# Softmax scores of a hybrid attention layer: float32 products replaced by three rounded products of split queries and keys

## The reference

```python
s = jnp.einsum('bhqd,bhkd->bhqk', q_blk, kh, preferred_element_type=jnp.float32) * scale
q_chunk = (blk * QBLOCK + jnp.arange(QBLOCK)) // CHUNK
mask = key_chunk[None, :] <= q_chunk[:, None]
p = jax.nn.softmax(jnp.where(mask, s, -1e30), axis=-1)
return jnp.einsum('bhqk,bhkv->bhqv', p.astype(vh.dtype), vh)
```

## Time and profile before

| | |
|---|---|
| median of 3 runs | 1137.3 us (1136.0 to 1137.32) |
| profiled execution | 1134.42 us |
| its span | 1132.3 us |
| TensorE busy | 1109.2 us (98%) |
| VectorE busy | 766.8 us (68%) |
| GpSimd busy | 529.7 us (47%) |
| ScalarE busy | 477.3 us (42%) |
| granted TensorE clock, mean | 0.998 |

### The profile page before, as it was taken

One profiled execution on the slowest core, in us unless ns is written; L12 is line 12 of the kernel. 1 busy time (PEld: TensorE's weight loads), 2 busy tenths in 40 slices (PEclk: granted clock), 3 DMA queues, 4 the chain that ended last, 5 costly groups with the idle time before them and its releaser, 6 DMA issues.

```text
span 1132.3 us, 14084 instructions
## 1 busy us (share of the span) xinstructions
PE 1109.2 (98%) x5094; PEld 874.6 (77%) x5094; DVE 766.8 (68%) x985; ACT 477.3 (42%) x869; POOL 529.7 (47%) x386
## 2 busy tenths in 40 slices
PE   7999999999999999999999999999999999999998
PEld 7978888764555558887888888888878888888887
DVE  5565767575575571288485775577798978888863
ACT  5353554426757562166323322332334434434341
POOL 2332613205475573047554444444545656555562
PEclk9999999999999999999999999999999999999999
DMA  7232523461221134223544234431789783456632
GB/s 255 66 130 75 168 85 112 108 164 36 75 62 52 57 115 164 75 86 101 177 142 138 101 112 139 139 113 38 262 276 377 236 285 121 135 192 216 208 116 84
DMA packets 101716, 158.37 MB, mean 140 GB/s; under 512 B 9360, under 2 KB 43232, under 8 KB 101648
## 3 DMA queue, kind: packets, MB, share of 16 engines
q1 hardware_dynamic: 100032, 152.83, 40.8%
q10 hardware_dynamic: 1296, 4.46, 1.1%
q0 software_dynamic: 320, 0.19, 0.2%
HBM read 115.47 MB, written 41.94 MB: 139 GB/s over the span
## 4 chain that ended last, share of the span: by engine, by line
PE 83%; DVE 8%; POOL 3%; issue 3%; DMA 2%; ACT 1%; SPq 0%; DVEq 0%; POOLq 0%; ACTq 0%
PE ps L2152 80%; POOL p_first L1022 1%; PE ps L2248 1%; DVE m_nm L1850 1%; DVE t_all L1924 1%; POOL tx_lo L1060 1%; DVE dr_lo L1924 1%; DMA up_raw<-in_w_up_dram 1%; DMA raw<-in_w_in_dram 1%; PE ps L2167 1%; POOL ua_lo L1065 1%; DMA m_ukv<-in_w_ukv_dram 0%; DVE stage L1924 0%; POOL a_lo L1060 0%; DVE xn L1564 0%
## 5 line engine op out<-in xcount | busy, mean ns | idle before, releaser
L2152 PE MATMUL ps<-dr_hi,dl_hi 128*128 128x512 f32 x448 | 174.5, 390 | 1.6 <-DVE dr_lo L1924 1.6
L2152 PE MATMUL ps<-dr_hi,dl_lo 128*128 128x512 f32 x448 | 174.3, 389 | 0.0
L2152 PE MATMUL ps<-dr_lo,dl_hi 128*128 128x512 f32 x448 | 174.3, 389 | 0.0
L1065 POOL TENSOR_TENSOR ua_lo<-up_raw,ua_hi 128x1024 fp32r<-128x1024 f32 x46 | 116.7, 2542 | 116.7 <-ACT ua_hi L1103 116.7
L1089 POOL TENSOR_TENSOR dl_lo<-l_raw,dl_hi 128x512 fp32r<-128x512 f32 x64 | 100.6, 1597 | 71.1 <-ACT dl_hi L1103 70.7
L1089 POOL TENSOR_TENSOR dl_lo<-s_all,dl_hi 128x512 fp32r<-128x512 f32 x48 | 75.2, 1586 | 58.2 <-ACT dl_hi L1103 57.5
L2152 PE MATMUL ps<-a_hi,ua_hi 128*128 128x512 f32 x256 | 99.9, 390 | 0.3 <-POOL ua_lo L1065 0.3
L2152 PEld LDWEIGHTS ps<-dr_hi,dl_hi 128*128 128x128 f32 x448 | 84.1, 188 | 20.1 <-issue 2.8
L2152 PE MATMUL ps<-a_hi,ua_lo 128*128 128x512 f32 x256 | 99.6, 389 | 0.0
L2152 PE MATMUL ps<-a_lo,ua_hi 128*128 128x512 f32 x256 | 99.6, 389 | 0.0
L2152 PEld LDWEIGHTS ps<-dr_lo,dl_hi 128*128 128x128 f32 x448 | 84.1, 188 | 17.5
(11 more groups left out here) (259 smaller groups left out, 2482.9 us busy)
## 6 DMA issues: line engine op xcount, KB each, us to landing
r_raw<-in_w_down_dram SPq DMA_DIRECT2D x144, 256.0 KB, 3.6
hidden<-stage SPq DMA_DIRECT2D x72, 256.0 KB, 2.1
up_raw<-in_w_up_dram SPq DMA_DIRECT2D x16, 1024.0 KB, 5.5
l_raw<-hidden SPq DMA_DIRECT2D x64, 256.0 KB, 3.5
raw<-in_w_in_dram SPq DMA_DIRECT2D x24, 256.0 KB, 3.4
z_gla<-z_stage SPq DMA_DIRECT2D x16, 256.0 KB, 2.0
raw<-in_w_out_dram SPq DMA_DIRECT2D x16, 256.0 KB, 3.3
xs<-in_x_dram SPq DMA_DIRECT2D x8, 512.0 KB, 7.3
```

What stands on the lines that cost most here:

```text
L1065: pool.tensor_tensor(ua_lo[n % UP_RING][:, :, :], up_source(g, product), ua_hi[n % UP_RING][:, :, :].bitcast(F32), ALU.subtract).then_inc( ...
L2152: return pe.matmul(dst, lhsT, rhs, start=start, stop=stop, skip_group_check=onto)
```

## The change

Scores are made of rounded factors. `m_q_hi` and `m_k_hi` get the 97th row (maxima and ones), `m_q` and `m_k` lose it, and in their place in memory stand `m_q_lo` and `m_k_lo` once the low parts are made. A score tile is three accumulated products: hi*hi with 97 rows, hi*lo and lo*hi with 96. Tiles of 128 queries are made 256 wide. The low parts are made by GpSimd (`mla_low`: four before `decays(0)`, and in step L0 of each pair but the last three for the next pair) and, for the queries of even units from the third on, by VectorE (`queries_low`, at step S1, place 2). A third row of ones is written by ScalarE. Of the odd unit's last three estimates, number 5 moves from place 0 of S0 to place 3 of the step L3 before it, number 6 stays at place 1, and number 7 goes from place 2 to place 3. The turn of the odd unit's maxima goes from S1 place 1 to place 2 for every pair, GLA part 1 (`gla_out`) from place 3 to place 2 of S0. Three pairs of semaphores are merged into single ones. The last denominators and the last GLA output go one block later into the output projection.

```diff
+        m_q, m_q_lo = ([at(f"{name}{n}", [DQK, 2, W], offset * KB, dt) for n, offset in enumerate((144, 168, 44, 60))]
+                       for name, dt in (("m_q", F32), ("m_q_lo", F32R)))
+        m_q_hi = [at(f"m_q_hi{n}", [DQK + 1, 2, W], offset * KB, F32R) for n, offset in enumerate((148, 200, 12, 28))]
...
-        ESTIMATES = {(S0, 0): (1, 5), (S0, 1): (1, 6), (S0, 2): (1, 7), (L0, 1): (2, 0), (L0, 3): (2, 1), (L1, 1): (2, 2),
-                     (L1, 2): (2, 3), (L2, 0): (3, 0), (L2, 1): (3, 1), (L2, 2): (3, 2), (L2, 3): (3, 3), (L3, 2): (3, 4)}
+        ESTIMATES = {(S0, 1): (1, 6), (S0, 3): (1, 7), (L0, 1): (2, 0), (L0, 3): (2, 1), (L1, 1): (2, 2),
+                     (L1, 2): (2, 3), (L2, 0): (3, 0), (L2, 1): (3, 1), (L2, 2): (3, 2), (L2, 3): (3, 3), (L3, 2): (3, 4),
+                     (L3, 3): (3, 5)}
...
-            if (d, place) == (1, 2):
-                return 1
-            if (d % 6, place) == (S1, 1) and d >= 6:
+            if (d % 6, place) == (S1, 2):
                 return 2 * (d // 6) + 1
...
-        GLA_AT = ((-1, 0, None, 1), (None, 2, None, None), (3, 4, None, 5), (6, 7, 8, 9), (10, 11, 12, None),
+        GLA_AT = ((-1, 0, 1, None), (None, 2, None, None), (3, 4, None, 5), (6, 7, 8, 9), (10, 11, 12, None),
...
+            def mla_low(kind, n):
+
+                pool.wait_ge(mla_hi, rounded(kind, n))
...
+                pool.tensor_tensor(at[:, :, some], whole[:, :, some], hi_at[0:DQK, :, some].bitcast(F32),
+                                   ALU.subtract).then_inc(m_lo_made, 1)
...
+            mla_low("k", 0)
+            mla_low("q", 0)
+            mla_low("k'", 0)
+            mla_low("q", 1)
             decays(0)
...
+                if t == L0 and p + 1 < MH // 2:
+                    mla_low("k", p + 1)
+                    mla_low("k'", p + 1)
+                    mla_low("q", 2 * p + 3)
...
+                if t == L1 and p == MH // 2 - 2:
+                    row_of_ones(2)
...
+            def queries_low(u):
+                n = queries_at(u)
+                dve.wait_ge(mla_hi, rounded("q", u))
+                for h in range(2):
+                    last = dve.tensor_tensor(m_q_lo[n][:, h, :], m_q[n][:, h, :], m_q_hi[n][0:DQK, h, :].bitcast(F32),
+                                             ALU.subtract)
+                last.then_inc(q_lo_made, 1)
...
+                    if (d % 6, place) == (S1, 2) and d // 6 + 1 < MH // 2:
+                        queries_low(2 * (d // 6) + 2)
...
-                seen = slice(first_query(j), W)
+                    pe.wait_ge(m_lo_made, LOW.index(("k'" if u % 2 else "k", p)) + 1)
+                    if ("q", u) in LOW:
+                        pe.wait_ge(m_lo_made, LOW.index(("q", u)) + 1)
+                    else:
+                        pe.wait_ge(q_lo_made, u // 2)
+                seen = slice(min(first_query(j), W - 2 * P), W)
+                some = slice(c * P, (c + 1) * P)
+                q, k = queries_at(u), keys_hi_at(p)
                 for s in range(2):
-                    last = mm(ps[:, score_bank(j) + s, seen], m_k[p % 2][:, s, c * P:(c + 1) * P],
-                              m_q[queries_at(u)][:, s, seen], True, True)
+                    to = ps[:, score_bank(j) + s, seen]
+                    mm(to, m_k_hi[k][:, s, some], m_q_hi[q][:, s, seen], True, False)
+                    mm(to, m_k_hi[k][0:DQK, s, some], m_q_lo[q][:, s, seen], False, False)
+                    last = mm(to, m_k_lo[p % 2][:, s, some], m_q_hi[q][0:DQK, s, seen], False, True)
...
-                    project(IN_GROUPS + n, pos, {(0, 0): last_sums, (0, 1): last_output}.get((n, pos)))
+                    project(IN_GROUPS + n, pos, {(0, 1): last_sums, (0, 2): last_output}.get((n, pos)))
```

More of the change, by code:

```diff
@@ L168, in layer @@
         m_v = at("m_v", [P, MH // 2, NB, 2 * MV], 128 * KB)
[L171 to L174, removed]
+        m_q, m_q_lo = ([at(f"{name}{n}", [DQK, 2, W], offset * KB, dt) for n, offset in enumerate((144, 168, 44, 60))]
+                       for name, dt in (("m_q", F32), ("m_q_lo", F32R)))
+        m_q_hi = [at(f"m_q_hi{n}", [DQK + 1, 2, W], offset * KB, F32R) for n, offset in enumerate((148, 200, 12, 28))]
+        m_k, m_k_lo = ([at(f"{name}{n}", [DQK, 2, T], offset * KB, dt) for n, offset in enumerate((152, 84))]
+                       for name, dt in (("m_k", F32), ("m_k_lo", F32R)))
+        m_k_hi = [at(f"m_k_hi{n}", [DQK + 1, 2, T], offset * KB, F32R) for n, offset in enumerate((192, 96, 128))]
         m_raw = [at(f"m_raw{u}", [P, W], (32 + 2 * (KT * (u % 2) + GH + u // 2)) * KB) for u in range(MH)]
         m_inv = [at(f"m_inv{u}", [P, W], 2 * (KT * (u % 2) + GH + u // 2) * KB) for u in range(MH)]
-        m_row = at("m_row", [NB, 2, P], 191 * KB)
+        m_row = at("m_row", [NB, 2, P], 191 * KB, F32R)
         ke_tok = at("ke_tok", [P, GH * GDK], 190 * KB)
@@ L335, in layer @@
         block = ctx.enter_context(nc.Block())
-        IDENT, FREQ, ONES = 1, 2, 3
+        IDENT, FREQ, ONES, ZEROS = 1, 2, 3, 5
         def x_landed(b, n):
@@ L560, in layer @@
             ROUNDED += [("q", 2 * _p + 2)] + [("ones", 1)] * (_p == 0) + [("k", _p + 1), ("k'", _p + 1), ("q", 2 * _p + 3)]
+        ROUNDED += [("ones", 2)]
         def rounded(kind, n):
             return 2 + ROUNDED.index((kind, n)) + 1
-        ESTIMATES = {(S0, 0): (1, 5), (S0, 1): (1, 6), (S0, 2): (1, 7), (L0, 1): (2, 0), (L0, 3): (2, 1), (L1, 1): (2, 2),
-                     (L1, 2): (2, 3), (L2, 0): (3, 0), (L2, 1): (3, 1), (L2, 2): (3, 2), (L2, 3): (3, 3), (L3, 2): (3, 4)}
+        LOW = [("k", 0), ("q", 0), ("k'", 0), ("q", 1)]
+        for _p in range(1, MH // 2):
+            LOW += [("k", _p), ("k'", _p), ("q", 2 * _p + 1)]
+        ESTIMATES = {(S0, 1): (1, 6), (S0, 3): (1, 7), (L0, 1): (2, 0), (L0, 3): (2, 1), (L1, 1): (2, 2),
+                     (L1, 2): (2, 3), (L2, 0): (3, 0), (L2, 1): (3, 1), (L2, 2): (3, 2), (L2, 3): (3, 3), (L3, 2): (3, 4),
+                     (L3, 3): (3, 5)}
         FIRST_ESTIMATES = {NB * IN_GROUPS - 3: {3: 0, 6: 1, 7: 2}, NB * IN_GROUPS - 2: {1: 3, 4: 4, 6: 5},
@@ L657, in maxima @@
                 sp.wait_ge(turned_out, u + 1)
-                sp.dma_start(m_q[queries_at(u)][DQK:DQK + 1, :, :].rearrange("o s (b n) -> o (s b) n", n=P),
-                             m_row[:, u % 2, :]).then_inc(q_in[u % 3], 16)
+                sp.dma_start(m_q_hi[queries_at(u)][DQK:DQK + 1, :, :].bitcast(F32).rearrange("o s (b n) -> o (s b) n", n=P),
+                             m_row[:, u % 2, :].bitcast(F32)).then_inc(q_in[u % 3], 16)
             def keys(p):
@@ L986, in _ @@
             pool.wait_ge(kT_out, NB)
-            pool.memset(sc[:, :, :], 0.0).then_inc(sc_zero, 1)
-            pool.memset(state[:, :, :, :], 0.0).then_inc(sc_zero, 1)
+            pool.memset(sc[:, :, :], 0.0).then_inc(const_ready, 1)
+            pool.memset(state[:, :, :, :], 0.0).then_inc(const_ready, 1)
             def decays(c):
@@ L996, in decays @@
                 pool.tensor_tensor(g_qf[:, c % 2, :, :], g_qf[:, c % 2, :, :], zq(c), ALU.mult).then_inc(qf_ready, 1)
+            def mla_low(kind, n):
+                pool.wait_ge(mla_hi, rounded(kind, n))
+                if kind == "q":
+                    at, hi_at, some = m_q_lo[queries_at(n)], m_q_hi[queries_at(n)], slice(0, W)
+                    whole = m_q[queries_at(n)]
+                else:
+                    at, hi_at, some = m_k_lo[n % 2], m_k_hi[keys_hi_at(n)], slice(0, W) if kind == "k" else slice(W, T)
+                    whole = m_k[n % 2]
+                pool.tensor_tensor(at[:, :, some], whole[:, :, some], hi_at[0:DQK, :, some].bitcast(F32),
+                                   ALU.subtract).then_inc(m_lo_made, 1)
             def mla_scale(u):
@@ L1294, in round_queries @@
                 n = queries_at(u)
-                copy(m_q_hi[n][:, :, :], m_q[n][0:DQK, :, :]).then_inc(mla_hi, 1)
+                copy(m_q_hi[n][0:DQK, :, :], m_q[n][:, :, :]).then_inc(mla_hi, 1)
             def round_keys(p, half):
@@ L1302, in round_keys @@
                 some = slice(half * W, (half + 1) * W)
-                copy(m_k_hi[keys_hi_at(p)][:, :, some], m_k[p % 2][0:DQK, :, some]).then_inc(mla_hi, 1)
+                copy(m_k_hi[keys_hi_at(p)][0:DQK, :, some], m_k[p % 2][:, :, some]).then_inc(mla_hi, 1)
             def row_of_ones(n):
                 act.wait_ge(const_ready, ONES)
-                row = m_k[n][DQK:DQK + 1, :, :].rearrange("o s (b n) -> o (s b) n", n=P)
+                row = m_k_hi[n][DQK:DQK + 1, :, :].rearrange("o s (b n) -> o (s b) n", n=P)
                 copy(row, ones[DQK:DQK + 1, :].unsqueeze(1).broadcast_to([1, 2 * NB, P])).then_inc(mla_hi, 1)
```

27 lines of the change are left out of this document (14 added, 13 removed).

## The result

The changed kernel takes 1154.3 us (median), the kernel before 1137.3: a ratio of 1.0143, with a 95% interval of 1.0109 to 1.0178. It is slower by 17.0 us, where 13.3 was forecast. The measured time lies 0.3 us above the upper end of the range. The profiled execution took 1154.13 us and the one of before 1134.42, so between the two traces there are 19.7 us to find (20.1 between the spans).

The account below looks back on a forecast made before the run. TensorE, busy 42.21 of 44 us per attention period, was taken to bound, its waits set by chains through the other engines. -6.9 + 9.7 + 1.0 + 3.0 + 6.1 + 0.4 = +13.3 on 1137.3 gave 1150.6 us, range 1131 to 1154.

Parts of the forecast that it names:

- scans behind GpSimd: At the start, VectorE's scaling and eight scans stand behind GpSimd's first four low parts: +9.7 us, bounds 0 to 9.7.
- clock behind that wait: At the start, TensorE's clock is lower after standing idle some 9 us: +1.0 us (0 to 1.7).
- copy of the maxima late: VectorE's copy stands behind `gla_lo`, delaying long units' scores: 2.7 us in second and third pair, 0.7 in last, +6.1 total.
- clock behind the maxima waits: Lower TensorE clock after the waits for the maxima before the long units' scores: nothing counted in the sum.
- products, less GpSimd's later low parts: Cheaper score products on TensorE, -6.9 us, with GpSimd's low parts in the first long steps, +3.0 (0 to 7.2).
- end: order: At the output projection, sums one block later: 1.0 us cost, 0.6 of slack saved, +0.4 us.
- clock behind the wait at the end: At the output projection, no lower clock counted; the earlier 1.53 us wait did nothing to the clock.
- they take turns: VectorE instructions with two SBUF operands and GpSimd's alternate, one each, the second standing still; applied to the scans, +9.7 us.
- Rival A: At the start, scans are not held in turns: 10.7 us become 0 to 4.7, total 1139.9 to 1144.6; chance 0.22.
- Rival B: GpSimd's work hides fully and the maxima come in time, nearly the whole TensorE gain stays: 1130.1 us; chance 0.22.
- rival C: Clock also falls behind the three waits for the maxima, 1.7 us each: 1155.7 us; chance 0.08.
- on the path: Attention products whose time counts: 22 tiles of 512 (-7.5) and three pairs of narrow ones (+0.6), -6.9 us.

Follow-up runs that it names:

- the kernel with the scans first: Against the changed kernel, GpSimd waits for the end of VectorE's running sums before its first four low parts: 1145.0 us, ratio 1.0065 to the kernel before.
- the held kernel: On top of both repairs, GpSimd's low part of the odd unit's queries waits for VectorE's two subtractions for the next decays: 1149.3 us, ratio 1.0108.
- both repairs: Changed kernel with GpSimd's first low parts after VectorE's scans, and VectorE's copy of the maxima ahead of `gla_lo`: 1134.8 us, ratio 0.9982.
- the filled gap: Changed kernel with 16 unused TensorE transposes made while the maxima are on their way, pairs two to four: 1150.1 us, ratio 1.0111.
- the two fastest kernels: Both repairs plus the odd unit's queries' low part on VectorE, 1132.4 us; scans first, old tables and sums' place, that low part on VectorE, 1132.3 us.

## Why the prediction was right and wrong

Direction and most mechanisms held; the clock behind the later waits was left out. Of 20.1 us between the spans, each term against what the traces give (the clock behind the maxima waits and the products are worked out as differences):

| term | predicted | by the traces |
|---|---|---|
| scans behind GpSimd | +9.7 | +8.6 |
| clock behind that wait | +1.0 | +1.5 |
| copy of the maxima late | +6.1 | +4.4 |
| clock behind the maxima waits | 0 | +5.5 |
| products, less GpSimd's later low parts | -3.9 | -2.2 |
| end: order | +0.4 | +0.4 |
| clock behind the wait at the end | 0 | +1.6 |

0.3 us of the rest of the span stay without a cause.

**The scans.** The step "they take turns" was the right reading of the earlier trace rows, and the kernel with the scans first shows it: with the clock behind it, 9.6 us in the trace. Some 1.5 us of scans lay behind the last GpSimd instruction (239.13 less 237.58), and the first began 0.6 us after GpSimd did, so the eight were drawn out by 8.4 and not by 9.7, and the estimate came 8.6 later. Rival A, in which the scans keep their turn, is out. The Trainium skill's rule (SBUF — State Buffer, "Who interferes with whom"), that a VectorE instruction with two SBUF inputs contends with a GpSimd instruction that reads SBUF, is borne out for a scan by 11.04 against 2.63 us. But "in turns, one instruction each" holds for the scans and not in general: the held kernel shows one VectorE instruction behind five of GpSimd's.

**The clock.** At S0 the delay is 10.1 and at the second estimate 8.6, so the clock behind the wait cost 1.5.

**The maxima.** Order and cause were as forecast: `a_lo` in front of the copy, 2.04 us idle on TensorE. Sizes: the first period grew by 2.12 us against that with both repairs (45.17 and 43.05), and from the estimate at 353.31 to the third long unit's scores it is 10.94 us against 8.84; so 2.1 twice in place of 2.7. In the last pair it is 2.94 us from the turn to the scores against 2.71, 0.2 in place of 0.7. I had made it 3.4 us from the end of ScalarE's rounding to the scores; it was 2.8 (309.94 to 312.70). Rival B, for which `a_hi` would have had to be early, is out: VectorE waited 2.12 for it.

**The clock behind them.** This is the step that failed. I set it to zero, because a wait of 1.53 us did nothing and the only lower clock had come behind 2.79; a wait of 2.0 to 2.7 lies between, and I left it out of the sum with a chance of 0.08 (rival C). It came once in the changed kernel's trace (7.7 in the period, less 2.1 of the wait at its end and 0.1 that the kernel with both repairs also loses: 5.5 us) and twice in that with the scans first. The rival was wrong in form, too: not 1.7 at each wait, but nothing at one and 5.5 at another. With the filled gap the clock stays up, and that period is 5.8 us shorter. Why one wait of 2.04 us is followed by the lower clock and the next is not stays open.

**Products and later low parts.** The tile measured 0.31 to 0.32 less in place of 0.34, and products of 256 columns start 0.12 apart, where I had 0.13. What was wrong is "on the path": of 6.9 us only 4.1 and 4.4 reach the path in the two fastest kernels, and TensorE waits for row maxima there. What makes these late once the low part is off GpSimd was not tested. The later low parts were priced at 3.0; taking one third of them off GpSimd gave 2.4 back, with VectorE's own 1.28 a pair still in it, so the price seems right or a little low. The two can't be divided further with these runs.

**The end.** The stretch cost the 0.4 that I had for the order, though only 0.27 of it goes by the order. The wait for the weights' low part was foreseen, its 2.23 us and the 1.6 of clock behind it, in some kernels and not in others, were not.

The profiled execution of before lay 2.9 us below its median and that of after on its median. Of the 6.4 us that the forecast missed between the traces, 3.7 are left between the medians. That it comes so near is in part luck: the scans and the maxima were priced 2.8 us too high together, which hid part of the 7.1 us of clock that stood at nothing.

## What to carry to other kernels

When work is given to an idle GpSimd, look at what VectorE does beside it: in these kernels an instruction with two operands in SBUF stood still for one or for several of GpSimd's, and where it stood mattered more than how much GpSimd did. A wait added to move such a collision must be checked against the next two-operand instruction, not only against the one it frees. And price a new wait of some 2 us on TensorE with the lower clock that can follow: of the twelve unfilled waits of 2.03 to 2.24 us in the changed kernels, seven were followed by one. Filling the wait is worth trying only where there is one; in the last pair it cost 1.5 us.

## What the runs showed of the hardware

- A VectorE instruction of 0.42 us with both operands in SBUF took 2.62 us beside one GpSimd instruction, and 6.54 to 6.56 us (four times, in two kernels) where GpSimd had five in a row. Of the eight scans, four got in one by one between GpSimd's four instructions (2.49 to 2.52 us each). What decides between the two wasn't found.
- A wait of 2.04 us on TensorE was followed by 16 us at 0.53 once and by 1.00 the next time in the same execution; waits of 2.21 to 2.24 us before the same instruction were followed by 1.00 in four kernels and by 0.79 over 8 us in four others. With sixteen transposes of 1.97 us in all put into the wait, the clock was 1.00 behind it both times.
- The clock's part differs from run to run: one of the changed kernel's four runs took 1149.3 us at a mean clock of 0.993, the others 1154.1 to 1156.4 at 0.984 or 0.985.
